# States past the last chunk left out, a chunk's products with zeros left out, and linear attention's key tiles, decay scans and factors reordered, in a two-block hybrid network

## The reference

```python
def step(s, xs):                          # GLA, one chunk
    ...
    o = einsum('bhid,bhde->bhie', qc * exp(b), s) + einsum('bhij,bhje->bhie', attn, vc)
    s_new = exp(b_last)[..., None] * s + einsum('bhjd,bhje->bhde', kc * exp(b_last - b), vc)
    return s_new, o
...
o_c, s_f, s_b = bidir_scan(gla_chunk_scan, sh_c, fw_c, bw_c, s0, s0)
o_l, _, _ = bidir_scan(gla_chunk_scan, sh_l, fw_l, bw_l, s_f, s_b)
```

## Time and profile before

| what | value |
|---|---|
| time of three runs | 3885.39, 3888.26, 3888.74 us (median 3888.26) |
| the profiled execution | 3874.18 us, of which the span of its instructions 3872.4 us |
| granted TensorE clock, mean | 0.981 of full speed |
| PE / PEld busy | 3709.1 us (96%) / 2366.5 us (61%) |
| DVE / ACT / POOL busy | 1749.7 us (45%) / 969.2 us (25%) / 610.7 us (16%) |
| DMA | 276.51 MB, mean 71 GB/s |

### The profile page before, as it was taken

One profiled execution on the slowest core, in us unless ns is written; L12 is line 12 of the kernel. 1 busy time (PEld: TensorE's weight loads), 2 busy tenths in 40 slices (PEclk: granted clock), 3 DMA queues, 4 the chain that ended last, 5 costly groups with the idle time before them and its releaser, 6 DMA issues.

```text
span 3872.4 us, 48478 instructions
## 1 busy us (share of the span) xinstructions
PE 3709.1 (96%) x19360; PEld 2366.5 (61%) x19360; DVE 1749.7 (45%) x3889; ACT 969.2 (25%) x1806; POOL 610.7 (16%) x551
## 2 busy tenths in 40 slices
PE   6999989978999999999999999999999999999999
PEld 3578874855467444444444468886764558976654
DVE  3877762255444133333333674622542273622531
ACT  4233322132100220000001611421552321322531
POOL 4001210041000132222222402311000101311001
PEclk8999989988999999999999999999999999999999
DMA  6301122145346111111110413311002221411021
GB/s 209 121 15 30 29 62 65 33 161 181 111 151 211 43 33 44 44 44 44 44 44 24 152 34 88 88 56 35 1 1 87 103 85 56 119 48 33 1 82 44
DMA packets 216109, 276.51 MB, mean 71 GB/s; under 512 B 27389, under 2 KB 174424, under 8 KB 215248
## 3 DMA queue, kind: packets, MB, share of 16 engines
q1 hardware_dynamic: 202336, 205.18, 17.1%
q0 software_dynamic: 13552, 68.24, 4.7%
HBM read 238.58 MB, written 34.81 MB: 71 GB/s over the span
## 4 chain that ended last, share of the span: by engine, by line
PE 86%; DVE 8%; ACT 3%; issue 2%; DMA 1%; POOL 0%; DVEq 0%; ACTq 0%; POOLq 0%
PE ps L3174 18%; PE ps L1049 10%; PE ps L3045 9%; PE ps L4135 6%; PE ps L1071 6%; PE ps L4427 4%; PE ps L4604 3%; PE ps L2803 3%; PE ps L4086 2%; PE ps L4661 2%; PE ps L4644 2%; PE ps L3242 1%; PE ps L1135 1%; PE ps L1824 1%; PE ps L1840 1%
## 5 line engine op out<-in xcount | busy, mean ns | idle before, releaser
L3174 PE MATMUL ps<-big 128*128 128x512 f32 x1624 | 697.1, 592 | 0.0
L3174 PEld LDWEIGHTS ps<-big 128*128 128x128 f32 x1624 | 308.6, 190 | 388.4 <-issue 385.3
L1049 PE MATMUL ps<-big 128*128 128x512 f32 (+1 forms) x1216 | 467.7, 545 | 1.7 <-DMA big<-hs_scratch 1.7
L1049 PEld LDWEIGHTS ps<-big 128*128 128x128 f32 x1216 | 230.7, 191 | 230.6 <-issue 223.5
L3045 PE MATMUL ps<-big 128*128 128x512 f32 (+1 forms) x896 | 359.3, 562 | 3.0 <-DVE big L4791 2.0
L3045 PEld LDWEIGHTS ps<-big 128*128 128x128 f32 x896 | 169.6, 190 | 187.7 <-issue 180.8
L3367 DVE SCALAR_TENSOR_TENSOR big<-ps,big 128x512 f32<-128x512 f32 x212 | 159.2, 751 | 242.6 <-PE ps L3174 208.7
L4135 PE MATMUL ps<-big 128*128 128x256 f32 x1152 | 252.7, 379 | 0.0
L1071 PE MATMUL ps<-big 128*128 128x256 f32 (+1 forms) x1344 | 229.9, 333 | 5.1 <-ACT big L2275 5.1
L4135 PEld LDWEIGHTS ps<-big 128*128 128x128 f32 x1152 | 217.0, 190 | 28.9 <-issue 0.4
L1071 PEld LDWEIGHTS ps<-big 128*128 128x128 f32 x1344 | 208.7, 192 | 25.6 <-ACT big L2275 5.5
(11 more groups left out here) (502 smaller groups left out, 5412.6 us busy)
## 6 DMA issues: line engine op xcount, KB each, us to landing
big<-in_w_mlp SPq DMA_DIRECT2D x32, 1024.0 KB, 5.4
big<-in_w_in SPq DMA_DIRECT2D x29, 1024.0 KB, 5.4
big<-in_w_mod SPq DMA_DIRECT2D x24, 1024.0 KB, 5.4
big<-in_w_ada SPq DMA_DIRECT2D x24, 1024.0 KB, 7.4
big<-us_scratch SPq DMA_DIRECT2D x72, 256.0 KB, 4.5
hs_scratch<-big POOLq DMA_DIRECT2D x3, 5120.0 KB, 17.3
big<-c_dft SPq DMA_DIRECT2D x12, 1024.0 KB, 5.6
xs_scratch<-big POOLq DMA_DIRECT2D x16, 640.0 KB, 3.5
```

The costliest lines, as they stand in the source:

```text
L1049: t = e.matmul(b[:, 0:n], wv[:, k, 128 * m:128 * m + 128], K.hT[:, k, t0:t0 + n], start=(k == 0), stop=(k == 7))
L3174: t = e.matmul(z, w[:, k, c], y, start=(first and k == 0), stop=(k == nk - 1), skip_group_check=not first)
```

## The change

1. At place 9, the last, the state is no longer updated: in GDN (PE products, DVE decay and add, POOL `kd`), in GLA (transposes of `kd`, the ACT copy, PE products, DVE adds) and in mLSTM of both layers (PE products, DVE adds, POOL weighted values).
2. In mLSTM's first layer, place 0 leaves out the products with the state (L4122), which is zero there.
3. GLA's projections: PE takes a and k block by block: a of block 0, both key tiles of block 0, a of blocks 1 and 2, both key tiles of block 1, GDN's transposes, both key tiles of block 2. ACT's copies follow that order.
4. DVE's log decays and scans are written between the copies of v's first 256 columns.
5. The factors of g = 0 and 1 (all but the "far" ones of g = 1) are written into GLA's projections: on DVE between the copies of v's last 128 columns, on ACT after `dec` and ahead of the output gate's Silu, on POOL ahead of the scan's `begin`. Only the far factors of g = 1 stay at the scan's start. The buffers of these factors are moved to memory that is free by then.

The core of the diff (the functions `factors_...` hold what stood inside the methods before):

```diff
@@ GdnTensor.state
-        u, kd, vn = self.key("S", d, c), ch["X"], ch["vn"]
-        b = self.pr.open(e, u)
...
+        if place < 9:
+            u = self.key("S", d, c)
+            b = self.pr.open(e, u)
+            e.wait_ge(*self.at(*self.key("kd", d, c)))
...
@@ GlaProj.tensor
-        for t0, n in BLKS:
...
-        self.cm(e, P, "k", 2, pr, then=lambda i: self.head.turned(e) if i == 0 else None)
+        a(0)
+        self.pair(e, P, "k", pr, wv, used, 0, 512, (0, 1))
+        a(1)
+        a(2)
+        self.pair(e, P, "k", pr, wv, used, 512, 512, (0, 1))
+        self.head.turned(e)
+        self.pair(e, P, "k", pr, wv, used, T, TC, (0, 1))
@@ GlaProj.scalar
+        for d, g, part in self.scan.early:
+            self.scan.factors_scalar(e, d, g, part)
         for c, nn, t in self.tm_each(384, range(8)):
@@ GlaProj.vector
+        between = {(0, 3): (decay, 0), (0, 4): (scan, 0, 0), (0, 5): (scan, 0, 1), (0, 6): (decay, 1),
+                   (0, 7): (scan, 1, 0), (0, 8): (scan, 1, 1)}
+        for i, (d, g, part) in enumerate(x for x in self.scan.early if x[2] == 0):
+            between[256, 2 * i] = (self.scan.factors_vector, e, d, g, part)
@@ GlaScan
+        self.early = [(0, 0, 0), (1, 0, 0), (0, 1, 0), (0, 1, 2), (1, 1, 0), (1, 1, 2)]
...
-        for g in range(2):
-            for d in range(2):
-                factors(d, g, 0)
-                factors(d, g, 1)
+        for d in range(2):
+            factors(d, 1, 3)
...
     def gpsimd(self, e):
+        for d, g, part in self.early:
+            self.factors_gpsimd(e, d, g, part)
         self.begin(e)
@@ GlaScan.tensor, second
+            if place == 9:
+                return
             u = key("S", d, c)
@@ MlScan.order
-                if place:
+                if 0 < place < 9:
                     s.state(d, place)
@@ MlTensor.near
-                e.matmul(b[:, o], X[:, hs], m.vtm[:, c, sl], start=True, stop=False)
-                t = e.matmul(b[:, o], Y[:, hs], Cs[:, sl], start=False, stop=True)
+                t = e.matmul(b[:, o], X[:, hs], m.vtm[:, c, sl], start=True, stop=(place == 0))
+                if place:
+                    t = e.matmul(b[:, o], Y[:, hs], Cs[:, sl], start=False, stop=True)
```

More of the change, by code:

```diff
@@ L1132, in pair @@
             b = ring.open(e, u)
+            self.ready(e, t0)
             for k in range(8):
@@ L2078, in right @@
         e, G, m, d, c = self.e, self.G, self.m, self.d, self.chunk(place)
-        if n == 6:
+        if n == 6 and place < 9:
             e.wait_ge(*self.at(*self.key("left", d, c, 6)))
@@ L2179, in __init__ @@
         self.At = [H1.get(2, 256) for _ in range(2)]
-        rem = Arenas([H1, C1])
-        self.work = {(d, q): {n: rem.get(512) for n in ("kd", "qs", "kk", "qd", "far")}
-                     for d in range(2) for q in range(2)}
+        early, late = Arenas([C1, spent]), H1
+        self.work = {(d, q): {n: (early if (q or n == "kd") and n != "far" else late).get(512)
+                              for n in ("kd", "qs", "kk", "qd", "far")} for d in range(2) for q in range(2)}
 class GlaProj(Proj):
-    def __init__(self, K, m, head, after):
+    def __init__(self, K, m, head, scan, after):
         super().__init__(K, "gla_in", "gla", after)
-        self.m, self.head = m, head
+        self.m, self.head, self.scan = m, head, scan
         self.blocks = [(d, p, t0, n) for d in range(2) for p in range(2) for t0, n in BLKS]
@@ L2467, in factors, with first @@
         def factors(d, g, part):
[L2468 to L2484 removed]
+            self.factors_scalar(e, d, g, part)
+        def first(d, place):
+            if place == 9:
+                return
             u = self.key("kdT", d, GDN_ORDER[d][place])
```

244 lines of the change are left out of this document (129 added, 115 removed).

## The result

| | before | changed |
|---|---|---|
| runs | 3885.39 to 3888.88 us, median 3888.50 (4 runs) | 3841.51 to 3845.88 us, median 3845.81 (4 runs) |
| the profiled execution | 3874.18 us (span 3872.4) | 3841.51 us (span 3839.7) |
| PE busy | 3709.1 us | 3693.8 us |
| granted clock, mean | 0.981 | 0.984 |

The ratio is 0.9889, with a 95% interval of 0.9872 to 0.9906: the changed kernel is faster by 1.1%, 42.7 us between the medians and 32.7 us between the two profiled executions. So the sum (31.3 us) fits the profiled executions and not the medians; that difference is the main subject of the experiments.

What follows compares the result with a forecast made beforehand. PE, busy 96% of the span, was taken to bound the kernel. Terms 3.8 + 5.7 + 5.1 + 9 + 2.8 + 1.3 + 3.6 = 31.3 us off 3888.3 gave a median of 3857 us, range 3848 to 3868 us.

Steps and rivals of the forecast that it cites:

- the sum: All terms of the change together: 31.3 us less, with bounds of 25.3 and 34 us.
- The step that failed: Whole program: the median's distance of 14.1 us above the profiled execution was carried over unchanged to the changed kernel.
- Part 1: GDN's last state left out: PE's products and DVE's decay and add go, 3.8 us, at least 2.4.
- Part 2: GLA's a and k block by block: PE's waits of 3.18 and 2.48 us for hT go, 5.7 us.
- Part 3: GLA's decay scans between v's copies: the output gate's stall of 5.13 us goes, at no cost.
- rival (b): Shorter waits raise the clock behind L592 and in GDN's tail, 2 us each: 3853 us; chance 0.10.
- Part 4: GLA scan's start: factors ready early, gain of 8 to 10 us, 9 taken, lower bound 6.
- The cheap end: GLA scan's start: DVE's half-size differences cost 0.4 us each, 1.6 us for both directions; dear end 1.0 each.
- rival (a): A wait replaces that of GLA scan's start or the gate's stall: 5 to 9 us lost; chance 0.16.
- Part 5: GLA's last state and two pairs of transposes left out: 2.8 us (2.0 to 3.4).
- Part 6: mLSTM: products with the zero state left out, 1.3 us; four last states in two layers, 3.6 us.
- Rival (c): Low clock behind hT's wait spreads over k, decay products, q, v; k and q alone give 3919 us; chance 0.03.

Runs made afterwards that it cites:

- e1: The unchanged kernel run again without an edit: median 3884.38 us (12 runs), profiled execution 3873.77 us.
- the first profile: The profiled execution of the changed kernel in the result table, 3841.51 us.
- e2: Kernel before plus only the last states and mLSTM's products with zeros left out: median 3871.23 us, ratio 0.9973.
- e5: The changed kernel again, no edit, second set of runs: median 3853.34 us (5 runs), ratio 0.9928.
- e6: The changed kernel with all factors back at GLA scan's start: median 3858.16 us, ratio 0.9943.
- e7: The changed kernel with 36 identity products as fill in GDN's scan: median 3852.83 us, ratio 0.9923.
- e9: The changed kernel a third time, no edit: median 3846.33 us (6 runs), ratio 0.9909.
- experiment 7: The changed kernel with two modulation steps moved into PE's wait for hT behind GLA's scan: median 3876.38 us, ratio 0.9982.
- experiment 4: Kernel before plus only the decay scans between v's copies, factors still at the scan's start: median 3877.31 us, ratio 0.9985.
- experiment 8: As experiment 7, plus twelve identity products filling the wait at the moved steps' old place: median 3859.29 us, ratio 0.9939.

## Why the prediction was wrong in its number and right in its parts

**The step that failed** is "The median of the runs, 3888.26 us, is 14.1 us above it; I carry that distance over unchanged". It took the distance between one execution and the median for a property of the program. It is mainly the granted clock in unchanged scan code, drawn anew in each execution: the profiled execution before (3874.18 us) was near the lowest time of its kernel, its three shown runs were in the upper half of its times, and the four runs of the changed kernel came from the low end of its own. The profiled execution was forecast at 3842.9 us and came at 3841.5. With all 87 and 15 runs the medians are 3883.9 and 3849.0 us, 34.9 us apart, against 31.3 forecast. The range was built from the bounds of the terms, with "a few microseconds of another chip" on top, and held no term for this spread of 19 us, which three runs within 3.4 us did not show; the profile's clock of 0.85 and 0.81 in GDN's scan was a hint of it, in a stretch that the change does not touch and the prediction does not speak of. That the new median fell below the range and not above it was the luck of which executions were timed: a second set of the same kernel had its median at 3853.3 us, inside the range, and a third at 3846.3 us, below it again.

**Part 1** (3.8 us, at least 2.4): 1.7 us on PE and 1.0 behind it, DVE's step; 2.7 us, between the bound and the term.

**Part 2** (5.7): both waits gone, 5.5 to 5.7 us when done alone. In the changed kernel 4.5 us, as a of block 0 took 6.46 us instead of 5.64 in e1: it ran at the lower clock for longer (0.50 over 580 to 586 us). The term had no such price.

**Part 3** (5.1): 7.0 and, alone, 6.8 to 7.0 us. The stall was right, the recovery behind it (0.72) was not in the sum. It is rival (b)'s mechanism at a place that the rival did not name.

**Part 4** (9, of 8 to 10): 10.2 us from the gate's last product to L592, shown in the traces by undoing it. The cheap end for the differences held; rival (a) named a real candidate, but DVE's eight inserts took 7.4 us, not 14.

**Part 5** (2.8): 3.4 us. 2.0 us come up to the last output, which is the forecast 0.68 + 0.8 and 0.5 more, and 1.4 us by the second block's first product, which is near the 1.35 us of DVE's adds. In the first profile they are not yet seen at the start of the Hyena input, as hT landed 10.8 us behind the last output's add instead of 9.5 us behind the adds of the state; in the other profiles without the last state (e2, e5, e6, e7, e9) PE starts it 10.4 to 10.6 us behind the last output instead of 11.8 to 12.6 us.

**Part 6** (1.3 + 3.6, which is 3.1 for the first layer and 1.8 for the second): 3.0 us in the first layer, of which 0.5 are lost again by the second scan, then 2.0 us in the second and 1.4 us behind it. The last is the clock (1.00 instead of 0.94), which the sum did not have. Alone (e2) the first layer gave only 1.4 us; why the two differ is open.

Put together, the parts are 2.7 + 4.5 + 7.0 + 10.2 + 3.4 + 5.9 us, less the 1.4 us that are no part of the change, so 32.3 us. Parts 1 and 2 came 1.1 and 1.2 us under their terms, parts 3, 4, 5 and 6 came 1.9, 1.2, 0.6 and 1.0 us above them. The sum of 31.3 us is closer than its terms, as these errors cancel.

**Rival (c)**, the low clock that spreads, did not come in the changed kernel at the place it names, but it came at others: in the changed kernel itself over 20 us of GLA's scan in one profile of three (e5), and in experiment 7, where it cost 15 us behind a new wait of 3.31 us. Its chance of 0.03 was for one place. The Trainium skill, "TensorE: Matmul & The Clock Gate", section "HAM oscillation — how this bites in real kernels", says that idle gaps throttle the array; experiments 4, 7 and 8 agree (0.72 behind an idle gap, 0.50 behind another, 1.00 when it is filled). It does not account for the 0.50 in GDN's scan, where PE was busy for all 15 us.

## What to carry to other kernels

Before a median is forecast from one profiled execution, look at the granted clock over the whole span, in windows, also where nothing changes: stretches below 1.00 with a busy PE are what varies between runs, and the forecast's range has to hold them. Price a wait of PE not by its length alone but with the clock behind it (here 5.1 us cost 6.8 to 7.0, and 3.3 us cost 15 more), and before filler work is moved out of a place, ask which wait it covers there. Compare kernels by stages of two traces that agree in the unchanged stretches, or by the runs with the same mean clock.

## What was not expected of the hardware

- The same instructions in GDN's scan ran in one execution at a granted clock of 1.00 throughout and in another at 0.50 for 15 us and 0.7 for 30 more, with PE busy 13.0 to 15.0 of each 15 us in both. What decides it in an execution is open.
- A wait of 3.31 us ahead of eight transposes and then 64-row products was followed by 39 us at 0.50. The longer waits of 5.13 us (ahead of the output gate's 128-row products) and of 10.02 us (ahead of a and k, 128 rows too) showed 0.72 over 6 us and 0.50 over 6 us, then 1.00 and 0.99. The wait of 3.93 us ahead of L592 (128 rows) had 0.83 over 10 us and then 1.00 behind it in four profiles, and 0.50 over 20 us in two. So the shape of the products behind the wait is not all of it, and whether it has a part was not tested by itself.
- The clamp on DVE (L2561), which has one input, took 0.43 us and, while POOL multiplied, 1.37 us. So not only DVE's differences of two inputs get dearer beside POOL. The Trainium skill, "SBUF — State Buffer", section "Who interferes with whom", has `tensor_scalar` among the operations that can take the port pair shared with GpSimd; the trace agrees. The prediction's sentence that by that page the inserts cost their dear price always was too strong: here they paid only where POOL was already at work.
- Two more megabytes of weights ahead of hT, in a stretch where the DMA engines moved 390 GB/s, brought PE's first product 4.8 us later than in the first profile and 6.2 us later than in four others, on either side of the 5.4 us that their size makes at that rate.
